# Cached samples on a table of uneven slots, four value pages a visit, and value rows spread by GpSimd

## The chip, the cores and the metric

One core of a Trainium2 chip runs the kernel. The metric is the device time of one execution in microseconds; lower is better. TensorE (PE in the profile), VectorE (DVE), ScalarE (ACT), GpSimd (POOL) and the DMA queues work at the same time, and each engine runs its own instruction list in order.

## The reference, cut to what matters

One step of a decoder layer, for a prompt of 256 tokens and for 8 samples of one token each (264 tokens together). Every token is projected by one large weight matrix. From the projections come two branches, attention with 8 heads and an mLSTM memory with 4 heads, which are gated, projected again and added to the input.

```python
xn = rms_norm(x, norm_w)
aq, ak, av, az, mq, mk, mv, mo, mz, ga, gm, mi, mf = split(xn @ w_in)
# attention of a sample over its 1024 cached tokens (8 pages of 128): the 3 best of 4 blocks of 256
gate = einsum(q, mean of each block's keys);  keep the top 3 blocks
p = softmax([q . k of the kept blocks, q . k_new]);  out = p @ [v, v_new]
# mLSTM, one sample (one token), per head:  C is 256 x 256, n is 256
c_new = a_prev * C + a_s * outer(k, v)          # all 8 samples x 4 heads are written back
n_new = a_prev * n + a_s * k
h     = (w_inter * q @ C + s * v) / max(|den|, exp(-m))
# mLSTM, prompt: the same over 256 tokens with decay weights w[s, t] (a cumulative sum along the row)
y = x + (sigmoid(ga) * ((attn * silu(az)) @ w_proj_attn) + sigmoid(gm) * ((h * silu(mz)) @ w_proj_mlstm)) @ w_out
```

The whole matrix is in fp32: 112 chunks of weights (1024 x 128, 512 KB each) are read once, and the keys and values of 64 pages (512 KB each) once.

## The kernel before, in words

Everything is laid out channel by token. A chunk of weights gives 128 channels of 264 tokens: the weights are split into a rounded part `whi` (ScalarE, L818) and the rest `wlo` (VectorE, L1071), and `project` (L506 to L538) does 16 matmuls with `whi` and 8 with `wlo`. One chunk is one **slot** here. The first 8 chunks are the query heads. Then come 64 slots of the body (g = 0 to 63, in four rounds j of 16, i = g modulo 16), and 40 slots of the tail (g = 64 to 103; i = 0 to 39 in the code of the tail).

Beside the projections each engine does the rest of the work at fixed slots, written out by hand in each engine's loop. On TensorE the extra work of two body slots is done together behind the projection of the odd slot (`beside`, L721, called at L743 to L748); in the tail it follows each slot (L790).

- **A round j** makes one mLSTM head and two attention heads (`keys_side`, `states_side`). At i = 8 TensorE reads the eight old states of the head against the samples' queries (L639), and at i = 9 it transposes the samples' value vectors, 8 rows of 256 (L645), and sums the prompt's normaliser (L652). ScalarE copies the value rows out twice, as fp32 and as rounded (L937, L938), VectorE makes the remainder (L1294, `mvs2`), and TensorE then spreads each sample's row over all 128 partitions by a matmul with a picked unit column (L689): four pairs of samples at i = 11, 12, 13 and 14, in the PSUM banks wk[0], wk[3], wk[0] and wk[2]. VectorE's `new_states` (L1245) takes the row from PSUM, multiplies it with the sample's key column and adds the faded old state (L1252), at i = 12, 13, 15 and at the next round's i = 0.
- **A cached sample b** has its eight key pages scored by VectorE, one a slot (`score_page`, L1162), from slot 2 + 9b. The lags SUMS to GATHER (L86) say what follows: sums on TensorE (L705), the choice of blocks on VectorE (`select`), a maximum over partitions on GpSimd (L462), shift, exp on ScalarE (`cache_probs`, L874), and the values on TensorE (L717), two pages a visit, four visits at lags 13, 15, 17 and 19. `gather` (L878) copies the result out.
- **GpSimd** issues the loads of key and value pages (L404). A key page may be loaded when VectorE has scored the one four pages back, and a value page when TensorE has used the one eight back. It also spreads the samples' query rows (L420) and the two decay rows of a round (L433, L434), which it first fetches from DRAM into partition 0 by DMA (L428, L429).

In-order waits tie these together: TensorE's norms at i = 1 and 3 of a round wait for `new_states` of the round before (L573, L576), since they write the same PSUM banks.

## Time and profile before

| | |
|---|---|
| median of 3 runs | 469.39 us (469.06 to 470.25) |
| span of the profiled execution | 467.2 us, 11345 instructions |
| PE, DVE, ACT, POOL busy | 456.2, 394.1, 294.4, 100.9 us |
| granted TensorE clock | 1.000 (2.4 GHz) over the whole span |
| DMA | 150.91 MB, mean 323 GB/s |

Of the profiled execution only the span, from its first to its last instruction, is known; its own time is not listed. The median of the timed runs is 2.2 us above that span.

The profile's rows give start and length of an instruction or of a run of equal ones. A matmul's end is modelled and reaches into the next, so lengths are read here from start to start. An fp32 matmul shows as two records, a rounded one (`project`) or a transpose as one.

### The profile page before, as it was taken

How to read it: one execution, taken by the hardware profiler on the slowest of the kernel's cores; microseconds unless marked ns; L12 is line 12 of the kernel's file. 1: busy time of each engine (PE TensorE's matmuls, PEld its weight loads, DVE VectorE, ACT ScalarE, POOL GpSimd, SP SyncE). 2: the span in 40 equal slices, each digit the busy share in tenths (PEclk: the TensorE clock that was granted, in tenths of full speed). 3: DMA queues.
4: the chain of work that ended last, by engine and by line, in shares of the span. 5: the costliest groups of instructions: out<-in, count | busy, mean ns of one | idle time of the engine just before them, and what ended most of it. 6: DMA issues, size and time to landing. Idle time of an engine off the chain costs nothing.

```text
span 467.2 us, 11345 instructions
## 1 busy us (share of the span) xinstructions
PE 456.2 (98%) x3855; PEld 413.8 (89%) x3855; DVE 394.1 (84%) x1610; ACT 294.4 (63%) x490; POOL 100.9 (22%) x181
## 2 busy tenths in 40 slices
PE   6999999999999999999999999999999999999997
PEld 4899899897879888888899889899898898899997
DVE  3898899699999799999899999799999774668861
ACT  4966545686984496995486695666948357324430
POOL 2040421013323213423321332321223110000000
PEclk9999999999999999999999999999999999999999
DMA  8899699749999999999999999998999985457511
GB/s 304 322 353 407 183 322 371 240 158 340 317 416 408 404 368 354 412 410 408 408 380 315 409 412 409 411 372 303 382 415 409 410 334 188 149 180 261 182 48 48
DMA packets 44858, 150.91 MB, mean 323 GB/s; under 512 B 6192, under 2 KB 7796, under 8 KB 44672
## 3 DMA queue, kind: packets, MB, share of 16 engines
q1 hardware_dynamic: 20368, 70.77, 40.8%
q0 software_dynamic: 19008, 67.20, 37.3%
q10 hardware_dynamic: 5424, 12.21, 6.8%
q8 instruction: 31, 0.51, 0.4%
q14 instruction: 27, 0.22, 0.1%
HBM read 137.37 MB, written 12.76 MB: 321 GB/s over the span
## 4 chain that ended last, share of the span: by engine, by line
PE 70%; ACT 10%; DVE 10%; DMA 4%; issue 4%; ACTq 1%; POOLq 0%; SPq 0%; POOL 0%; DVEq 0%
PE pj L534 28%; PE pj L537 13%; PE wk L534 6%; PE pa L717 4%; PE wk L537 3%; DMA kpages<-in_cache_k 3%; DVE kpages L1170 3%; DVE wlo L1071 2%; ACT L838 2%; ACT whi L818 2%; PE wk L487 2%; DVE cslot L1252 2%; PE wk L639 2%; PE wk L673 1%; DMA cst<-in_consts 1%
## 5 line engine op out<-in xcount | busy, mean ns | idle before, releaser
L534 PE MATMUL pj<-xn,whi 128*128 128x264 f32 x1328 | 180.8, 288 | 1.6 <-ACT mqT L976 1.3
L534 PEld LDWEIGHTS pj<-xn,whi 128*128 128x128 f32 x1328 | 168.4, 189 | 10.2 <-issue 6.2
L1071 DVE TENSOR_TENSOR wlo<-wraw,whi 128x1024 fp32r<-128x1024 f32 x112 | 136.1, 1220 | 8.8 <-ACT whi L818 8.3
L818 ACT ACTIVATE whi<-wraw 128x1024 fp32r<-128x1024 f32 x112 | 117.9, 1053 | 23.1 <-PE wk L537 12.9
L1170 DVE CUSTOM_DVE_ANT_0 kpages<-kpages,qbc 128x128 f32<-128x128 f32 x512 | 115.5, 292 | 5.3 <-DMA kpages<-in_cache_k 5.1
L537 PE MATMUL pj<-xn,wlo 128*128 128x264 f32 x664 | 93.8, 284 | 0.4 <-DVE wlo L1071 0.4
L537 PEld LDWEIGHTS pj<-xn,wlo 128*128 128x128 f32 x664 | 85.5, 188 | 0.6 <-DVE wlo L1071 0.6
L404 POOL DMA_DIRECT2D kpages<-in_cache_k x64 | 34.3, 536 | 165.9 <-DVE sco L1170 141.9
L404 POOL DMA_DIRECT2D vpages<-in_cache_v x64 | 33.9, 530 | 57.9 <-issue 38.9
L1170 DVE DVE_READ_ACCUMULATOR2_ANT sco<- 128x1 f32 x512 | 42.8, 84 | 0.0
L717 PE MATMUL pa<-vpages,prob 128*32 128x256 f32 x512 | 34.2, 385 | 1.7 <-ACT prob L876 1.7
L1252 DVE SCALAR_TENSOR_TENSOR cslot<-wk,kc,cslot 128x256 f32<-128x256 f32 x64 | 26.5, 478 | 1.7 <-PE wk L689 1.7
L534 PE MATMUL wk<-xn,whi 128*128 128x264 f32 x192 | 26.0, 288 | 0.0
L534 PEld LDWEIGHTS wk<-xn,whi 128*128 128x128 f32 x192 | 24.2, 189 | 1.6 <-issue 1.6
L717 PEld LDWEIGHTS pa<-vpages,prob 128*32 128x32 f32 x512 | 13.4, 109 | 13.6 <-issue 3.1
L866 ACT ACTIVATE cslot<-cslot,bcg 128x512 f32<-128x512 f32 x32 | 21.2, 711 | 0.0
L911 ACT ACTIVATE att<-att,rsum 128x128 f32<-128x128 f32 x8 | 3.2, 403 | 25.7 <-DVE rsum L1233 25.7
L534 PE MATMUL wk<-mlg,whi 128*128 128x264 f32 x128 | 17.0, 285 | 0.0
L534 PEld LDWEIGHTS wk<-mlg,whi 128*128 128x128 f32 x128 | 16.0, 188 | 0.5 <-issue 0.4
L534 PE MATMUL pj<-mlg,whi 128*128 128x264 f32 x112 | 14.9, 285 | 0.0
L534 PEld LDWEIGHTS pj<-mlg,whi 128*128 128x128 f32 x112 | 14.0, 188 | 0.8 <-issue 0.4
L537 PE MATMUL wk<-xn,wlo 128*128 128x264 f32 x96 | 13.5, 283 | 0.0
(271 smaller groups left out, 615.0 us busy)
## 6 DMA issues: line engine op xcount, KB each, us to landing
wraw<-in_weights SPq DMA_DIRECT2D x112, 512.0 KB, 6.8
kpages<-in_cache_k POOLq DMA_DIRECT2D x64, 512.0 KB, 8.1
vpages<-in_cache_v POOLq DMA_DIRECT2D x64, 512.0 KB, 10.8
cslot<-in_states SPq DMA_DIRECT2D x16, 512.0 KB, 9.4
out_C_s<-cslot ACTq DMA_DIRECT2D x16, 512.0 KB, 8.1
xres<-in_tokens SPq DMA_DIRECT2D x1, 1056.0 KB, 5.5
out_k_p<-kT ACTq DMA_DIRECT2D x4, 256.0 KB, 10.2
out_v_p<-v_nat ACTq DMA_DIRECT2D x4, 256.0 KB, 4.7
```

Source lines behind the costliest of these rows:

```text
L404: return pool.dma_start(tile, src)
L487: return nc.tensor.transpose(out, in_, ident[0:rows_, 0:rows_])
L534: mm(bank[:, 0:T], whi[:, q, k, :], src[:, g, k, :], start=(k == 0 and g == 0), stop=False)
L537: last = mm(bank[:, 0:T], wlo[:, n % WRAW, k, :], src[:, 0, k, :], start=False, stop=(k == KC - 1))
L639: mm(wk[1][g * VC:(g + 1) * VC, 0:MHD], qmask[:, d, b * VC:(b + 1) * VC], cslot[:, b, d, :], start=(half == 0 and d == 0), stop=(half == 1 ...
L717: last = mm(pv[q * VC:(q + 1) * VC, 0:VW], prob[:, b % 2, first:first + VC], vpages[:, s % VSLOTS, q * VW:(q + 1) * VW], start=(pg == 0), ...
L818: A(whi[:, n % WSPLIT], wraw[:, n % WRAW], ACT.Copy).then_inc(whi_ready, 1)
L838: ch.link(A(dst, ss, ACT.Ln, scale=1.0 / width, bias=epsc))
L866: A(cslot[:, b], cslot[:, b], ACT.Copy, scale=bcg[:, 0, j, b:b + 1]).then_inc(fade_ready, 1)
L1071: V.tensor_tensor(wlo[:, n % WRAW], wraw[:, n % WRAW], whi[:, n % WSPLIT], ALU.subtract).then_inc(wlo_ready, 1)
L1170: last = V.tensor_tensor_reduce(k, k, qbc[:, b % 2, h * HD:(h + 1) * HD], 1.0, 0.0, ALU.mult, ALU.add, sco[:, b % 2, pg, h:h + 1])
L1252: last = V.scalar_tensor_tensor(out=cslot[:, b, d, :], in0=row, scalar=kc[:, d, b:b + 1], in1=cslot[:, b, d, :], op0=ALU.mult, op1=ALU.add)
```

## The change

- **The samples' table.** `due`, `key_page` and the pairs of value pages no longer follow one period. Samples 0 to 5 start at slots 2, 12, 20, 30, 38 and 48, with the same lags as before; samples 6 and 7 have their keys over slots 58 to 66 and 68 to 78, and their other steps listed by hand. Values come in two visits of four pages, at 13 and 17 slots after the start, and for samples 6 and 7 at 74 and 77, 83 and 84. Value pages are loaded one a slot by a table of its own (`LOADS`).
- **Value rows.** The broadcasts by matmul (L689), the split (L938, L1294) and the two small transposes (L645) go. At i = 8 TensorE makes sixteen matmuls of 32 x 128 with the identity, each of a quadrant of 32 partitions, so that quadrant q of wk[3] holds the rows of samples 2q and 2q + 1. ScalarE copies that once into `mvq`, and GpSimd spreads one quadrant's first row (512 numbers) over 128 partitions into `mvb`, four times a round: two at i = 10, one at i = 12, one at i = 13. `new_states` reads the row from `mvb` in SBUF, no longer from PSUM.
- **Decay rows** are put once at the start into partitions 0, 32, 64 and 96 of a tile `stage`, by one DMA, and spread from there at i = 13; the DMAs of each round through DRAM go.
- **Order and waits.** The normaliser's sums (L652) go before the new matmuls in wk[1]; `nnew` is copied by VectorE (it was ScalarE). TensorE's norms wait for `pT_ready` and `cn_ready` of the round before, no longer for `new_states`. In the tail the tokens' scores move from slot 3 to 8 (TensorE), their VectorE part from 12 to 18, their exp from 14 to 19, the totals from 18 to 20. Some waits of GpSimd for its own results are added. The mask of the attention shares one copy, so the constants are 128 columns shorter.

```diff
-START, PERIOD = 2, 9
-SUMS, SELECT, SHIFT, EXP, VALUES, TOTAL, GATHER = 9, 10, 11, 12, 13, 14, 20
+SUMS, SELECT, SHIFT, EXP, TOTAL, GATHER = range(6)
+LAGS = (9, 10, 11, 12, 14, 20)
+STARTS = [2, 12, 20, 30, 38, 48]
+KEYS = [[s + p for p in range(PAGES)] for s in STARTS] + [[58, 59, 60, 61, 62, 63, 64, 66], [68, 69, 71, 72, 74, 75, 77, 78]]
+STEPS = [[s + lag for lag in LAGS] for s in STARTS] + [[68, 69, 70, 71, 72, 80], [79, 80, 81, 81, 82, 85]]
+VISITS = [[s + 13, s + 17] for s in STARTS] + [[74, 77], [83, 84]]
+LOADS = [[]] + [[s + 14 + p for p in range(PAGES)] for s in STARTS] + [[75, 76, 76, 77, 78, 78, 79, 79]]
...
-            def decay_rows(j):
+            def spread_rows(j):
...
-                pool.dma_start(wt[0:1, 0:SEQ], rows_dram[j:j + 1, 0:SEQ]).then_inc(row_load, 16)
-                pool.dma_start(emt[0:1, :], rows_dram[j:j + 1, SEQ:2 * SEQ]).then_inc(row_load, 16)
...
+                row = stage[j * VC:j * VC + 1, :]
+                nc.gpsimd.partition_broadcast(wt[:, 0:SEQ], row[:, 0:SEQ]).then_inc(row_spread, 1)
+                nc.gpsimd.partition_broadcast(emt, row[:, SEQ:2 * SEQ]).then_inc(row_spread, 1)
+                pool.wait_ge(row_spread, 2 * (j + 1))
+
+            def spread_values(j, c):
+
+                pool.wait_ge(mv_ready, 2 * j + 2)
+                if c >= 2:
+                    pool.wait_ge(c_ready, NB * j + 2 * (c - 1))
+                elif j:
+                    pool.wait_ge(c_ready, NB * (j - 1) + 2 * (c + 3))
+                nc.gpsimd.partition_broadcast(mvb[:, c % 2, 0:2 * MHD], mvq[c * VC:c * VC + 1, :]).then_inc(v_spread, 1)
+                pool.wait_ge(v_spread, VG * j + c + 1)
...
-                        pe.wait_ge(c_ready, NB * j - 2) if j else pe.wait_ge(q_ready, HEADS)
+                        pe.wait_ge(pT_ready, 2 * j) if j else pe.wait_ge(q_ready, HEADS)
...
-                        pe.wait_ge(c_ready, NB * j) if j else pe.wait_ge(qs_ready, 2)
+                        pe.wait_ge(cn_ready, j) if j else pe.wait_ge(qs_ready, 2)
...
-                    for n in range(2):
-                        last = tr(wk[3][0:NB, n * P:(n + 1) * P], rawT[:, n, SEQ:T], P)
-                    last.then_inc(mvtr_ps, 1)
...
+                    for pick in range(2):
+                        for n in range(2):
+                            c = pick * MHD + n * P
+                            for q in range(VG):
+                                col = SEQ + 2 * q + pick
+                                last = mm(wk[3][q * VC:(q + 1) * VC, c:c + P], rawT[:, n, col:col + 1].broadcast_to([P, VC]), ident,
+                                          start=True, stop=True)
+                    last.then_inc(mvtr_ps, 1)
...
-                if i in (11, 12, 13, 14):
-                    pair = i - 11
-                    bank = (wk[0], wk[3], wk[0], wk[2])[pair]
...
-                    for n in range(2):
-                        last = mm(bank[:, n * MHD:(n + 1) * MHD], eye2[:, 2 * pair + n:2 * pair + n + 1].broadcast_to([P, P]),
-                                  mvs2[:, :], start=True, stop=True)
-                    last.then_inc(vbc_ps, 1)
...
-                    for pg in (2 * pair[1], 2 * pair[1] + 1):
+                    for pg in range(many * p, many * (p + 1)):
...
+                    act.wait_ge(mvtr_ps, 2 * j + 2)
+                    act.wait_ge(v_spread, VG * j)
+                    A(mvq[:, :], wk[3][:, :], ACT.Copy).then_inc(mv_ready, 1)
...
-                    A(mvs, wk[3][0:NB, 0:MHD], ACT.Copy)
-                    A(mvs2[0:NB, :], wk[3][0:NB, 0:MHD], ACT.Copy).then_inc(mv_ready, 1)
-                    A(nnew[:, j, :], wk[3][:, MHD:MHD + MHD // VG], ACT.Copy).then_inc(n_ready, 1)
...
-                    dve.wait_ge(vbc_ps, 4 * j + b // 2 + 1)
-                    row = (wk[0], wk[3], wk[0], wk[2])[b // 2][:, b % 2 * MHD:(b % 2 + 1) * MHD]
+                    dve.wait_ge(v_spread, VG * j + b // 2 + 1)
+                    row = mvb[:, b // 2 % 2, b % 2 * MHD:(b % 2 + 1) * MHD]
...
+                    V.tensor_copy(nnew[:, j, :], wk[1][:, NNEW:NNEW + MHD // VG]).then_inc(n_ready, 1)
...
-                if i == 10:
-                    dve.wait_ge(mv_ready, 2 * j + 2)
-                    V.tensor_tensor(mvs2[LO:LO + NB, :], mvs, mvs2[0:NB, :], ALU.subtract).then_inc(mvlo_ready, 1)
```

How the instructions stand now. First TensorE behind the projection of slot 25 (second round, i = 8 and 9), in the kernel before; L639 reads the old states, L717 is a visit of two value pages, L645's transposes show under the helper's line L487 as `8x128`, and L652 is the normaliser:

```order
L487 MATMUL wk<-cst,att 128x128 x3
L487 MATMUL wk<-cst,sq 128x128 x4
L639 MATMUL wk<-cslot,qmask 32x256 x16
L641 MATMUL wk<-qsum,cst 128x16
L717 MATMUL pa<-vpages,prob 32x256 x8
L487 MATMUL wk<-cst,sq 8x128 x2
L652 MATMUL wk<-mk_nat,decay 32x64 x8
```

The same place in the changed kernel, with its own line numbers (L654 is the reading of the states, L670 the new matmuls, L721 a visit):

```order
L502 MATMUL wk<-cst,att 128x128 x3
L502 MATMUL wk<-cst,sq 128x128 x4
L654 MATMUL wk<-cslot,qmask 32x256 x16
L661 MATMUL wk<-mk_nat,decay 32x64 x8
L670 MATMUL wk<-cst,sq 32x128 x16
L673 MATMUL wk<-qsum,cst 128x16
L721 MATMUL pa<-vpages,prob 32x256 x16
```

The two transposes have become sixteen narrow matmuls, and the visit has twice as many matmuls.

Then TensorE in the tail, slots 78 to 80 of the kernel before, where L534 and L537 are projections:

```order
L534 MATMUL wk<-xn,whi 128x264 x16
L537 MATMUL wk<-xn,wlo 128x264 x8
L717 MATMUL pa<-vpages,prob 32x256 x8
L534 MATMUL wk<-xn,whi 128x264 x16
L537 MATMUL wk<-xn,wlo 128x264 x8
L534 MATMUL pj<-mlg,whi 128x264 x16
L537 MATMUL pj<-mlg,wlo 128x264 x8
L717 MATMUL pa<-vpages,prob 32x256 x8
```

And slots 83 and 84 of the changed kernel (L549 and L552 are projections, L766 the totals):

```order
L549 MATMUL wk<-mlg,whi 128x264 x16
L552 MATMUL wk<-mlg,wlo 128x264 x8
L721 MATMUL pa<-vpages,prob 32x256 x16
L549 MATMUL pj<-mlg,whi 128x264 x16
L552 MATMUL pj<-mlg,wlo 128x264 x8
L766 MATMUL wk<-lsum,cst 128x64
L721 MATMUL pa<-vpages,prob 32x256 x16
```

The tail had ten visits of two pages and has five of four.

Last GpSimd at the end of the first round, before (L420 spreads a query row, L428 and L429 fetch the decay rows, L433 and L434 spread them, L401 and L404 issue a page):

```order
L420 ISA qbc<-qbc 128x1024
L428 DMA decay<-rows_dram 1x16x16
L429 DMA floor<-rows_dram 1x16x16
L401 TENSOR_LOAD ptab
L401 ISA x2
L404 ISA
L404 DMA kpages<-in_cache_k 128x1024
L433 ISA decay<-decay 128x256
L434 ISA floor<-floor 128x256
```

and now, from slot 12 to 13 (L448 spreads two value rows, L437 and L438 the decay rows):

```order
L448 ISA mvb<-mvq 128x512
L408 TENSOR_LOAD ptab
L408 ISA x2
L411 ISA
L411 DMA kpages<-in_cache_k 128x1024
L448 ISA mvb<-mvq 128x512
L437 ISA decay<-stage 128x256
L438 ISA floor<-stage 128x256
```

The value rows' broadcasts stand between the loads of pages, and the decay rows need no DMA.

## Rows read from the trace of the kernel before

**Rows 1.** Page, part 1: busy time, share of the span, instructions
```profile
PE 456.2 (98%) x3855; PEld 413.8 (89%) x3855; DVE 394.1 (84%) x1610; ACT 294.4 (63%) x490; POOL 100.9 (22%) x181
```

**Rows 2.** Waits of TensorE in body and tail: us in total, times, longest
```profile
PE pa L717 <- ACT prob L876: 1.7, 3, 0.7
PE pj L534 <- ACT mqT L976: 1.3, 2, 0.7
...
PE pj L537 <- DVE wlo L1071: 0.4, 1, 0.4
```

**Rows 3.** Timeline of TensorE, slots 77 to 80: start us, length us
```profile
379.95 2.12 PE L534 MATMUL pj<-xn,whi 128*128 128x264 f32 x16
...
382.88 2.12 PE L534 MATMUL wk<-xn,whi 128*128 128x264 f32 x16
...
385.89 1.07 PE L717 MATMUL pa<-vpages,prob 128*32 128x256 f32 x16
386.89 2.23 PE L534 MATMUL wk<-xn,whi 128*128 128x264 f32 x16
...
389.93 2.12 PE L534 MATMUL pj<-mlg,whi 128*128 128x264 f32 x16
```

**Rows 4.** Timeline of TensorE, value rows of the third round, first and last pair
```profile
243.24 0.58 PE L689 MATMUL wk<-mvs,eye 128*128 128x256 f32 x2
243.66 2.13 PE L534 MATMUL pj<-xn,whi 128*128 128x264 f32 x16
...
258.33 0.40 PE L689 MATMUL wk<-mvs,eye 128*128 128x256 f32 x2
258.56 1.05 PE L696 MATMUL wk<-sq,cst 128*128 128x264 f32 x4
```

**Rows 5.** Timeline of TensorE, i = 8 and 9 of the fourth round
```profile
301.38 1.93 PE L639 MATMUL wk<-cslot,qmask 128*32 128x256 f32 x32
303.25 0.40 PE L641 MATMUL wk<-qsum,cst 128*128 128x16 f32 x2
...
303.74 0.38 PE L487 MATMUL wk<-cst,sq 128*8 128x128 f32 x2
304.05 0.43 PE L652 MATMUL wk<-mk_nat,decay 128*32 128x64 f32 x16
304.30 1.05 PE L717 MATMUL pa<-vpages,prob 128*32 128x256 f32 x16
```

**Rows 6.** Timeline of GpSimd, broadcasts of 256 and of 1024 numbers a partition
```profile
52.90 0.55 POOL L434 PARTITION_BROADCAST floor<-floor  x1
...
53.84 2.35 POOL L451 PARTITION_BROADCAST qbc<-qs  x1
...
157.28 1.45 POOL L420 PARTITION_BROADCAST qbc<-qbc  x1 [6.37 <-DMA qbc<-q_dram]
```

**Rows 7.** Timeline of VectorE, under the last of these
```profile
157.28 0.29 DVE L1170 CUSTOM_DVE_ANT_0 kpages<-kpages,qbc 128x128 f32<-128x128 f32 x1
...
157.49 1.24 DVE L1170 CUSTOM_DVE_ANT_0 kpages<-kpages,qbc 128x128 f32<-128x128 f32 x1
```

**Rows 8.** Groups of instructions, VectorE: busy us, mean ns, idle before
```profile
L1170 DVE CUSTOM_DVE_ANT_0 kpages<-kpages,qbc 128x128 f32<-128x128 f32 x512 | 115.5, 292 | 5.3 <-DMA kpages<-in_cache_k 5.1
L1252 DVE SCALAR_TENSOR_TENSOR cslot<-wk,kc,cslot 128x256 f32<-128x256 f32 x64 | 26.5, 478 | 1.7 <-PE wk L689 1.7
L1294 DVE TENSOR_TENSOR mvs<-zraw,mvs 8x256 fp32r<-8x256 f32 x4 | 2.0, 506 | 1.9 <-ACT mvs L938 1.9
```

**Rows 9.** Timeline of TensorE, slot 15
```profile
109.81 1.25 PE L537 MATMUL pj<-xn,wlo 128*128 128x264 f32 x8 [0.39 <-DVE wlo L1071]
```

**Rows 10.** Timeline of ScalarE, slots 30 to 34
```profile
187.48 0.39 ACT L881 ACTIVATE accr<-pa 128x256 f32<-128x256 f32 x1 [2.22 <-PE pa L717]
...
203.99 0.37 ACT L976 ACTIVATE mqT<-pj 128x264 f32<-128x264 f32 x1
```

**Rows 11.** Loads of pages by GpSimd (L404)
```profile
DMA to landing us min/median/max: 4.3/9.5/16.9
```

More of the change, by code:

```diff
@@ L77, with due, value_visit, value_loads @@
 VC = 32
+NNEW = MHD + VC
 BODY = JOBS * CHUNKS
 LAST = BODY + 5 * KC
-START, PERIOD = 2, 9
-SUMS, SELECT, SHIFT, EXP, VALUES, TOTAL, GATHER = 9, 10, 11, 12, 13, 14, 20
-def due(g, lag):
-    b, left = divmod(g - START - lag, PERIOD)
-    return b if left == 0 and 0 <= b < NB else None
-def key_page(g):
-    b, pg = divmod(g - START, PERIOD)
-    return b * PAGES + pg if 0 <= b < NB and pg < PAGES else None
-def value_pair(g):
-    for p in range(PAGES // 2):
-        b = due(g, VALUES + 2 * p)
-        if b is not None:
-            return b, p
-    return None
+SUMS, SELECT, SHIFT, EXP, TOTAL, GATHER = range(6)
[5 more added lines that the diff above has]
+LOADS = [[]] + [[s + 14 + p for p in range(PAGES)] for s in STARTS] + [[75, 76, 76, 77, 78, 78, 79, 79]]
+def due(g, step):
+    for b in range(NB):
+        if g == STEPS[b][step]:
+            return b
+    return None
+def key_page(g):
+    for b in range(NB):
+        if g in KEYS[b]:
+            return b * PAGES + KEYS[b].index(g)
+    return None
+def value_visit(g):
+    for b in range(NB):
+        for p, slot in enumerate(VISITS[b]):
+            if g == slot:
+                return b, p, PAGES // len(VISITS[b])
+    return None
+def value_loads(g):
+    return [b * PAGES + p for b in range(1, NB) for p in range(PAGES) if g == LOADS[b][p]]
 class Chain:
@@ L320, in build @@
         q_dram = nc.dram_tensor("q_dram", (NB, D), F32, kind="Internal").ap()
-        rows_dram = nc.dram_tensor("rows_dram", (MH, 2 * SEQ), F32, kind="Internal").ap()
         block = ctx.enter_context(nc.Block())
@@ L443, in _ @@
             pool.wait_ge(rows_ready, 1)
-            pool.dma_start(rows_dram, rows[:, :, :].rearrange("p a t -> p (a t)")).then_inc(row_put, 16)
+            pool.dma_start(stage[ds(0, MH, step=VC), :], rows[:, :, :].rearrange("p a t -> p (a t)")).then_inc(row_put, 16)
             pool.wait_ge(row_put, 16)
-            decay_rows(0)
             spread_rows(0)
@@ L470, in _ @@
                         spread_queries(s // PAGES + 1)
-                pair = value_pair(g)
-                if pair is not None:
-                    for s in range(pair[0] * PAGES + 2 * pair[1] + VSLOTS, pair[0] * PAGES + 2 * pair[1] + VSLOTS + 2):
-                        if s < NB * PAGES:
-                            values(s)
+                for s in value_loads(g):
+                    values(s)
+                if g < BODY and g % CHUNKS == 10:
+                    spread_values(g // CHUNKS, 0)
+                    spread_values(g // CHUNKS, 1)
+                if g < BODY and g % CHUNKS in (12, 13):
+                    spread_values(g // CHUNKS, g % CHUNKS - 10)
                 if g % CHUNKS == 13 and g // CHUNKS + 1 < JOBS:
-                    decay_rows(g // CHUNKS + 1)
-                if g % CHUNKS == 14 and g // CHUNKS + 1 < JOBS:
                     spread_rows(g // CHUNKS + 1)
@@ L640, in states_side @@
                                    start=(half == 0 and d == 0), stop=(half == 1 and d == EC - 1))
[L641 to L646 removed]
+                    pe.wait_ge(w_ready, j + 1)
                     part = MHD // VG
@@ L651, in states_side @@
                         for q in range(VG):
-                            last = mm(wk[3][q * VC:(q + 1) * VC, MHD:MHD + part], wt[:, col:col + 1].broadcast_to([P, VC]),
+                            last = mm(wk[1][q * VC:(q + 1) * VC, NNEW:NNEW + part], wt[:, col:col + 1].broadcast_to([P, VC]),
                                       mk_nat[:, t, q * part:(q + 1) * part], start=(t == 0), stop=(t == 1))
                     last.then_inc(n_ps, 1)
+                    pe.wait_ge(sw_ready, j + 1)
+                    for pick in range(2):
[6 more added lines that the diff above has]
+                    last.then_inc(mvtr_ps, 1)
+                    mm(wk[1][:, MHD:MHD + 2 * NB], ones, qsum[:, :, :], start=True, stop=True).then_inc(qc_ps, 1)
                 if i == 10:
@@ L705, in cache_side @@
                     mm(page_sums[b % 2], ones, sco[:, b % 2].rearrange("p a h -> p (a h)"), start=True, stop=True).then_inc(g_ps, 1)
-                pair = value_pair(g)
-                if pair is not None:
-                    b = pair[0]
-                    if pair[1] == 0:
+                visit = value_visit(g)
+                if visit is not None:
+                    b, p, many = visit
+                    if p == 0:
                         pe.wait_ge(prob_ready, b + 1)
                         pe.wait_ge(accr_ready, b)
-                    for pg in (2 * pair[1], 2 * pair[1] + 1):
+                    for pg in range(many * p, many * (p + 1)):
                         s = b * PAGES + pg
@@ L1402, in _ @@
                     merged_values()
[L1403 removed]
+                if i == 18:
                     token_scores()
```

69 lines of the change are left out of this document (23 added, 46 removed).

## The prediction

> **What bounds the kernel now.** I read the page's busy times first, then TensorE's waits, then its timeline from start to start, and last the engines that could take its place. TensorE is busy for 456.2 of 467.2 us, VectorE for 394.1, GpSimd for 100.9 [rows 1]. From the body on TensorE stands still for only 1.7 + 1.3 + 0.4 = 3.4 us in six waits of note, of which 3.0 us are waits for ScalarE [rows 2]. So two things can shorten this kernel: less work on TensorE, which counts in full wherever no other engine is late, and those 3.4 us. VectorE is close behind. In slot 15 TensorE waited for the weight remainder `wlo` [rows 9], so there VectorE had no lead left at all; it is the engine to fear.
>
> The profiled span is 467.2 us and the median of the runs 469.39. I make the sum against the span and carry the 2.2 us between them over unchanged.
>
> **Value rows: what TensorE loses and gains.** Eight matmuls L689 a round go. The first pair of the third round takes 243.66 - 243.24 = 0.42 us, the last 258.56 - 258.33 = 0.23 [rows 4]; the two between take 0.4 and 0.34, about 1.4 us a round and 5.6 in all. Not all of it is gained. L689 is of the same rounded kind as the projections, and softens the change between kinds. The cost of such a change shows in the tail: a slot alone lasts 382.88 - 379.95 = 2.93 us, the one that follows an fp32 visit 389.93 - 386.89 = 3.04, so 0.11 [rows 3]. Two to three places a round now pay it: 0.3 a round, 1.2 in all. The two transposes take 304.05 - 303.74 = 0.31 a round, 1.2 in all [rows 5].
>
> Added are sixteen fp32 matmuls of 32 x 128 a round. The trace has none of that shape. The nearest rows are those of L639, also 32 partitions wide, four quadrants in turn: sixteen of 256 columns in 303.25 - 301.38 = 1.87 us [rows 5]. Half the columns gives 0.94. L717 gives the same, eight of 256 columns in 386.89 - 385.89 = 1.00 [rows 3], so 1.0. From below, eight of 64 columns (L652) take 0.25 [rows 5], so sixteen take 0.5 if columns don't count. From above, if the quadrants did not overlap, each would cost what one of the two transposes does, 0.155, so 2.5 a round. I take 0.95, since L639 is the row that it is nearest to: 3.8 in all, between 2 and 10. Value rows together: -5.6 + 1.2 - 1.2 + 3.8 = -1.8 us, between -3.6 and +4.4.
>
> **Visits.** 32 visits of two pages become 16 of four; the matmuls stay 256. In the tail the slots 78 and 79 with a visit take 389.93 - 382.88 = 7.05 us against 2 x 2.93 = 5.86, so a visit of 1.00 brings 0.19 of change with it [rows 3]. Ten such visits stand in the tail before and five after: -0.95. In the body 22 become 11, all behind other fp32 work that pays most of the change anyway. I take 0.1 each, between 0 and 0.19: -1.1 (0 to -2.1). Visits together -2.0 us.
>
> **Waits.** The waits for ScalarE are at the seams of the rounds, where it has a chain of table loads. In the second seam it first waited 2.22 us at L881 for a visit of TensorE, then worked without a pause until the evacuation L976 at 203.99 that TensorE was waiting for [rows 10]. `gather` of that sample moves from slot 31 to 32 behind a visit of slot 29, so this wait goes, though its copy and two DMA issues now stand in the crowded slot. The exp of sample 6 (slot 68) goes to 72, off its visit. In the first seam ScalarE waits for VectorE's hidden state, and VectorE has no key page in slots 10 and 11 where it had one in 11. But both seams are chains on ScalarE, and what TensorE saves ahead of them is partly lost in waiting for them: about 1.5 us of value rows and visits lies in the stretches before. Of the 3.4 us I count 0.8 gained net; between 3.4 gained and nothing, with the TensorE savings there lost as well (+1.5).
>
> **VectorE.** It loses L1294, 2.0 us, and the wait ahead of it, 1.9, and the waits of L1252 for L689, 1.7 [rows 8]. Of the 56 key pages that it scored in the body 54 are left, which is 2 x 8 x 0.21 = 3.4 us (0.21 from start to start, 157.28 to 157.49 [rows 7]). It gains four copies of 64 columns, under 1 us together. I cost this at nothing because TensorE's own work hides it, save in slots like 15.
>
> Against it stand sixteen new broadcasts on GpSimd. One of 256 numbers takes 0.55 us, one of 1024 took 2.35 from another tile and 1.45 in place [rows 6]; 512 numbers lie between, 0.8 by the row in place. What such a broadcast does to VectorE the trace shows once clearly. Under L420 at 157.28 a scoring instruction took 1.24 us, where the mean is 0.29 [rows 6, 7, 8], so 0.95 lost. From below it is nothing, when VectorE is waiting anyhow or reads PSUM. I take 0.45 each, about half of the one row as the broadcast has half the length: 7.2 us against the 8 us of relief, so no net change. VectorE's L1252 reads its row from SBUF now instead of PSUM; its length (0.478) I leave alone.
>
> On this the Trainium skill has a rule that speaks against the change (SBUF — State Buffer, "Who interferes with whom"): a VectorE instruction with two SBUF inputs contends with a GpSimd instruction that reads SBUF, and whichever comes first locks the other out for its whole length. The stretched row agrees, as both of its inputs are in SBUF. By the rule L1252, whose row came from PSUM, joins those that can be locked out, and every broadcast that meets VectorE costs it what is left of the broadcast.
>
> **GpSimd's own queue.** The new broadcasts wait for ScalarE's copy (slot 10) and for `new_states` (slots 12, 13). Behind them in the queue are page loads. A key page is loaded four pages ahead and takes 4.3 to 16.9 us, 9.5 in the middle [rows 11]. Value pages of samples 2 and 4 are loaded only four slots before their visit. A slot lasts at least 2.93 us [rows 3], so they have at least 11.7 us and, with the work beside the projections, more. I cost it at nothing; if that cover is gone, a visit waits up to 16.9 - 11.7 = 5.2 us. GpSimd is 22% busy and eight DMAs of its queue go. The table's effect on ScalarE is two table loads fewer, in the tail where it waits for TensorE anyway: nothing. The end after the last projection is untouched, and so is the start, but for 64 KB of constants.
>
> **Sum.** -1.8 - 2.0 - 0.8 = -4.6 us. Span 462.6, time 464.8 us.
>
> **Rivals.**
> - *VectorE is held up by the broadcasts, and TensorE by it (slower).* For it: rows 7, and slot 15 without a lead [rows 9]. The place is i = 10 to 14 of each round, four broadcasts. At 0.95 each they cost 3.8 us a round, against 0.9 of L1294 with its wait and 0.85 of a key page; the 2.0 that is left reaches TensorE through `wlo`, 8 in all. With -3.8 of less work: +4.2, 473.6 us. The break-even is at (3.8 + 7.0) / 16 = 0.68 us a broadcast; above that the kernel is slower. Against it: VectorE is idle for some of that time, and two of the four come before the point at i = 11 where it waits for TensorE.
> - *ScalarE's seams set the rounds (no change).* For it: 3.0 of 3.4 us of waits are for ScalarE, and it is not relieved. Then the savings of the body become waits at the seams, and the tail's 0.95 alone is sure: 468.4 us. Against it: no single one of these waits is over 0.7 us.
> - *The waits go as well (faster still).* VectorE's free slots 10, 11, 28, 29, 46 and 47 put the hidden state and the shift early: -3.8 - 3.4 = -7.2, 462.2 us.
> - *Late value pages.* Two visits wait some 3 us each: -4.6 + 6 = +1.4, 470.8 us. Against it: before, pages landed in 9.5 us in the middle, and no visit waited for a DMA.
>
> **How the numbers follow.** Forecast 0.58 (463.4 to 467), the seams 0.13, the waits too 0.15, VectorE held up 0.11, late pages 0.03. Less or more than 0.3% (1.4 us) is what a measurement of this kernel can tell from no change. Faster: 0.58 + 0.15 and a share of the seams' case that saves more than 1.4 us, 0.77. Same 0.11, slower 0.12. The range of 80% runs from 461.8, the forecast with its waits gone, to 468.6, the seams' case. It leaves out most of the slower cases and the best ends of the value rows.
>
> **What would show it.** Right: no L689; the sixteen new matmuls of a round in about 0.95 us from start to start; visits of 2.0 us, 0.19 of change each, five in the tail; TensorE busy for about 452 of 463 us; its waits in the body no more than 3 us. Wrong: the new matmuls in 2 us or more; VectorE instructions of over 1 us under most of the L448 broadcasts, with waits of TensorE for `wlo`; waits of visits for a page; or waits at `mqT` or `prob` of more than 3.4 us together.

## The result, and the profile after

The changed kernel takes 475.61 us (median, 474.25 to 477.23) against 469.82 for the kernel before in the same comparison: ratio 1.0128, 95% interval 1.0107 to 1.015. The forecast was 464.8 us, the range 461.8 to 468.6. The sign is wrong and the time lies outside the range. The profiled execution took 475.26 us, its span 473.6.

The page of the changed kernel, parts 1 and 2, answers to [rows 1]: busy us, share of the span and instructions; then the granted clock of TensorE in 40 slices of 11.8 us, in tenths.

```profile
PE 454.1 (96%) x3943; PEld 418.1 (88%) x3943; DVE 397.7 (84%) x1610; ACT 291.7 (62%) x480; POOL 117.2 (25%) x185
...
PEclk9999999999999999997999999899999999999999
```

TensorE is busy for 2.1 us less than before, not 4, and there are two slices in which it ran at a lower clock. Its waits in the body and the tail, to be laid beside [rows 2] (us in total, times, longest):

```profile
PE pa L721 <- DMA vpages<-in_cache_v: 6.2, 2, 3.2
PE pa L721 <- ACT prob L881: 2.5, 2, 1.9
...
PE pj L552 <- DVE wlo L1074: 1.3, 3, 0.6
PE pj L549 <- ACT sq L839: 1.3, 1, 1.3
PE pj L549 <- ACT mqT L979: 1.1, 1, 1.1
...
PE wk L502 <- ACT att L917: 0.2, 1, 0.2
```

They sum to 12.6 us. Before, the same kinds of wait came to 3.8: the three of [rows 2], and two of 0.2 us. The first line is new. No visit waited for a page before; now two do, three microseconds each. The timeline of TensorE around them (start us, length us, and in brackets what it waited for):

```profile
206.12 2.12 PE L549 MATMUL pj<-xn,whi 128*128 128x264 f32 x16
208.08 1.13 PE L552 MATMUL pj<-xn,wlo 128*128 128x264 f32 x8
...
209.80 1.50 PE L721 MATMUL pa<-vpages,prob 128*32 128x256 f32 x24
214.32 1.08 PE L721 MATMUL pa<-vpages,prob 128*32 128x256 f32 x8 [3.02 <-DMA vpages<-in_cache_v]
215.33 3.89 PE L549 MATMUL pj<-xn,whi 128*128 128x264 f32 x16
219.02 1.72 PE L552 MATMUL pj<-xn,wlo 128*128 128x264 f32 x8
220.58 2.10 PE L549 MATMUL pj<-xn,whi 128*128 128x264 f32 x16
...
297.45 1.50 PE L721 MATMUL pa<-vpages,prob 128*32 128x256 f32 x24
302.18 1.08 PE L721 MATMUL pa<-vpages,prob 128*32 128x256 f32 x8 [3.23 <-DMA vpages<-in_cache_v]
303.19 3.31 PE L549 MATMUL pj<-xn,whi 128*128 128x264 f32 x16
306.34 1.13 PE L552 MATMUL pj<-xn,wlo 128*128 128x264 f32 x8
```

Three pages of the visit are used (x24), then TensorE stands still for the fourth: the last page of sample 2, and of sample 4. What follows is slow too. From start to start the sixteen L549 after the first wait take 219.02 - 215.33 = 3.69 us, the eight L552 1.56; after the second wait the L549 take 3.15. In a kernel below, in which the first wait is short, the same rows take 2.07 and 0.97, and the last eight matmuls of the visit 0.57 instead of 1.01. So after each wait some matmuls ran at the lower of the two clock levels, 1.2 instead of 2.4 GHz (the granted clock from 215.33 to 219.02 is 0.50 of full speed), and that cost (3.69 - 2.07) + (1.56 - 0.97) + (3.15 - 2.07) + 2 x (1.01 - 0.57) = 4.2 us. The windows of the trace show the granted clock there (length, busy time with instructions, clock as a share, DMA share, GB/s):

```profile
192.00:208.00 16.00, 14.85 (x131) 1.00 1.03 414
208.00:224.00 16.00, 12.98 (x99) 0.79 1.02 408
288.00:304.00 16.00, 12.77 (x109) 0.94 1.03 410
304.00:320.00 16.00, 16.00 (x183) 0.95 0.90 354
```

The span grew by 6.4 us: waits +8.8, lower clock +4.2, and so TensorE's own work -6.6. I call what is left of a span without those waits and that clock the kernel's work: 463.4 us before, 456.8 after. It is good to a few tenths only, since a listed wait leaves out what the matmuls lose at its edges (a case is read below, under the value rows alone). The work was forecast to shrink by 3.8 and shrank by more.

Why the page was late stands in GpSimd's timeline. These are slots 32 and 33:

```profile
196.18 0.53 POOL L411 DMA_DIRECT2D kpages<-in_cache_k  x1 [3.06 <-DVE sco L1173]
196.73 1.30 POOL L427 PARTITION_BROADCAST qbc<-qbc  x1
199.25 0.55 POOL L411 DMA_DIRECT2D vpages<-in_cache_v  x1 [1.22 <-issue]
201.67 0.53 POOL L411 DMA_DIRECT2D kpages<-in_cache_k  x1 [1.87 <-DVE sco L1173]
202.81 0.54 POOL L411 DMA_DIRECT2D vpages<-in_cache_v  x1 [0.61 <-issue]
```

The last two lines are slot 33: a key load that waits until VectorE has scored the page in its buffer (`sco`), and behind it the value load for slot 37. It leaves at 202.81 and lands at about 214.2, which is 11.4 us, a usual time for a page ([rows 11]: 9.5 in the middle, up to 16.9; the value pages of the changed kernel alone: 10.9 in the middle). TensorE wants it at 211.3. GpSimd keeps step with VectorE, and VectorE is some slots behind TensorE: TensorE had ended its visit of slot 33 at 194.93. The "four slots ahead" of the table are four slots in the order of the code; in time they were 8.5 us.

### The profile page after: what moved, and what is told of

It reads as the page before. It is cut to its first block, busy times and chain, and to the rows that moved or that the text cites. A ratio compares the mean times of both kernels' runs of the same rounds, so it can differ in the third digit from the quotient of the medians.

```text
span 473.6 us, 11533 instructions
## 1 busy us (share of the span) xinstructions
PE 454.1 (96%) x3943; PEld 418.1 (88%) x3943; DVE 397.7 (84%) x1610; ACT 291.7 (62%) x480; POOL 117.2 (25%) x185
## 4 chain that ended last, share of the span: by engine, by line
PE 70%; DVE 13%; ACT 6%; DMA 6%; issue 3%; POOL 1%; POOLq 0%; ACTq 0%; SPq 0%; DVEq 0%
PE pj L549 26%; PE pj L552 13%; PE wk L549 8%; DMA vpages<-in_cache_v 5%; PE pa L721 4%; PE wk L552 4%; DVE kpages L1173 3%; DVE wlo L1074 3%; PE wk L502 2%; DVE cslot L1255 2%; PE wk L654 2%; ACT L843 1%; ACT whi L823 1%; PE wk L558 1%; PE wk L557 1%
## 5 line engine op out<-in xcount | busy, mean ns | idle before, releaser
L549 PE MATMUL pj<-xn,whi 128*128 128x264 f32 x1328 | 184.4, 292 | 2.4 <-ACT sq L839 1.3
L549 PEld LDWEIGHTS pj<-xn,whi 128*128 128x128 f32 x1328 | 171.6, 191 | 9.6 <-issue 4.5
L1173 DVE CUSTOM_DVE_ANT_0 kpages<-kpages,qbc 128x128 f32<-128x128 f32 x512 | 118.9, 296 | 0.9 <-DMA kpages<-in_cache_k 0.7
L552 PE MATMUL pj<-xn,wlo 128*128 128x264 f32 x664 | 94.6, 285 | 1.3 <-DVE wlo L1074 1.3
L552 PEld LDWEIGHTS pj<-xn,wlo 128*128 128x128 f32 x664 | 86.1, 189 | 2.0 <-DVE wlo L1074 2.0
L1173 DVE DVE_READ_ACCUMULATOR2_ANT sco<- 128x1 f32 x512 | 41.2, 81 | 0.0
L721 PE MATMUL pa<-vpages,prob 128*32 128x256 f32 x512 | 32.2, 390 | 8.8 <-DMA vpages<-in_cache_v 6.2
L721 PEld LDWEIGHTS pa<-vpages,prob 128*32 128x32 f32 x512 | 15.1, 110 | 20.6 <-DMA vpages<-in_cache_v 7.2
L1255 DVE SCALAR_TENSOR_TENSOR cslot<-mvb,kc,cslot 128x256 f32<-128x256 f32 x64 | 27.2, 485 | 0.0
L549 PE MATMUL wk<-xn,whi 128*128 128x264 f32 x192 | 25.8, 287 | 0.0
L549 PEld LDWEIGHTS wk<-xn,whi 128*128 128x128 f32 x192 | 24.3, 189 | 1.2 <-issue 1.2
L549 PE MATMUL wk<-mlg,whi 128*128 128x264 f32 x128 | 17.1, 286 | 0.0
L448 POOL PARTITION_BROADCAST mvb<-mvq x16 | 16.5, 1032 | 0.8
L549 PEld LDWEIGHTS wk<-mlg,whi 128*128 128x128 f32 x128 | 16.2, 189 | 0.1
L1287 DVE COPY qcs<-wk 128x256 f32<-128x256 f32 x4 | 1.7, 422 | 17.2 <-PE wk L673 17.2
L549 PE MATMUL pj<-mlg,whi 128*128 128x264 f32 x112 | 15.1, 287 | 0.0
## 6 DMA issues: line engine op xcount, KB each, us to landing
vpages<-in_cache_v POOLq DMA_DIRECT2D x64, 512.0 KB, 10.9
```

The source lines that it names most:

```text
L448: nc.gpsimd.partition_broadcast(mvb[:, c % 2, 0:2 * MHD], mvq[c * VC:c * VC + 1, :]).then_inc(v_spread, 1)
L549: mm(bank[:, 0:T], whi[:, q, k, :], src[:, g, k, :], start=(k == 0 and g == 0), stop=False)
L552: last = mm(bank[:, 0:T], wlo[:, n % WRAW, k, :], src[:, 0, k, :], start=False, stop=(k == KC - 1))
L721: last = mm(pv[q * VC:(q + 1) * VC, 0:VW], prob[:, b % 2, first:first + VC], vpages[:, s % VSLOTS, q * VW:(q + 1) * VW], start=(pg == 0), ...
L1173: last = V.tensor_tensor_reduce(k, k, qbc[:, b % 2, h * HD:(h + 1) * HD], 1.0, 0.0, ALU.mult, ALU.add, sco[:, b % 2, pg, h:h + 1])
L1255: last = V.scalar_tensor_tensor(out=cslot[:, b, d, :], in0=row, scalar=kc[:, d, b:b + 1], in1=cslot[:, b, d, :], op0=ALU.mult, op1=ALU.add)
```

## The experiments

Two theories at the start. A: the two late pages, with the clock behind them, are the loss. B: the broadcasts hold VectorE up, and TensorE waits behind it. Ratios are to the kernel before, beside which each kernel ran (469.25 to 469.76 us), with 95% intervals. Diffs are against the changed kernel or the kernel before, as said.

### Value loads two a slot (against the changed kernel)

```diff
-LOADS = [[]] + [[s + 14 + p for p in range(PAGES)] for s in STARTS] + ...
+LOADS = [[]] + [[s + 14 + p // 2 + p // 4 * 2 for p in range(PAGES)] for s in STARTS] + ...
```

> The changed kernel with its value pages loaded two a slot instead of one (the first four of a sample at 14 and 15 slots after the start of the one before, the last four at 18 and 19), so that the last page has two slots more before its visit. Late-pages theory: the two waits for a value page (6.2 us) go, and with them the stretches of 1.2 GHz behind them (about 3.3 us by the rows of the changed kernel): 475.6 - 9.5 = about 466 us, clock 1.00. Broadcast theory (VectorE held up by GpSimd): nothing of its cost changes, 474 us or more.

467.92 us, ratio 0.9959 (0.9937 to 0.9981): 7.7 us faster than the changed kernel, and faster than the kernel before. No visit waits for a page and the clock stays up. A holds for most of the loss, though 2 us more stayed than I expected.

### The value rows alone (the changed kernel with the old table)

```diff
+STARTS = [2 + 9 * b for b in range(NB)]
+VISITS = [[s + 13, s + 15, s + 17, s + 19] for s in STARTS]
+LOADS = [[]] + [[VISITS[b][p // 2] for p in range(PAGES)] for b in range(NB - 1)]
 (KEYS, STEPS and the tail's steps as before the change)
```

> The changed kernel with the table of the kernel before (period of 9, visits of two pages, loads at the visits, tail steps at their old slots): only the value rows by GpSimd, the staged decay rows and the looser waits are new. Late-pages theory: no visit waits for a page; TensorE has some 1.8 us less work, and the broadcasts cost nothing: 466 to 468.5 us. Broadcast theory: the loss is here, 473 us or more.

471.34 us, 1.0024 (1.0009 to 1.004). I had expected 466 to 468.5 from A and 473 or more from B; it is neither. Its first line of waits is this:

```profile
PE pj L552 <- DVE wlo L1074: 4.7, 8, 1.1
```

### The same without the broadcasts

```diff
-                nc.gpsimd.partition_broadcast(mvb[:, c % 2, 0:2 * MHD], mvq[c * VC:c * VC + 1, :]).then_inc(v_spread, 1)
-                pool.wait_ge(v_spread, VG * j + c + 1)
+                pool.sem_inc(v_spread, 1)
 (and mvb is set to zero once at the start)
```

> As the run with the old table and the new value rows, but without the sixteen broadcasts of value rows: the semaphore is raised, the copy in SBUF stays at zero, so the outer product of the samples' new states is left out of the result. The difference to that run is the price of the broadcasts. Late-pages theory: under 0.5 us. Broadcast theory: 4 us or more faster than that run.

468.45 us, 0.9973 (0.996 to 0.9987), and the line is now

```profile
PE pj L552 <- DVE wlo L1074: 1.1, 1, 1.1
```

The sixteen broadcasts cost 471.34 - 468.45 = 2.9 us, and TensorE's listed waits for `wlo` fall from 4.7 to 1.1. B is real too, at 0.18 us a broadcast. It stands below the 4 us that B named, above the 0.5 of A. The list shows such a wait too short. At the second one (0.57 us, slot 17) a projection and the `wlo` matmuls behind it last 121.05 - 117.28 = 3.77 us from start to start, without the broadcasts 2.92, so 0.85 is lost. By this, a part of what the broadcasts cost hides in what I call work.

### The new table alone, value rows by matmul (against the kernel before)

```diff
-START, PERIOD = 2, 9
+STARTS = [2, 12, 20, 30, 38, 48]
 (KEYS, STEPS, VISITS and LOADS as in the changed kernel)
```

> The kernel before with the changed kernel's table (starts, keys, visits of four pages, loads one a slot, tail steps), and its value rows still by matmul. Late-pages theory: the loss is here, waits for value pages at the visits of slots 37 and 55 of some 3 us each and a lower clock behind them: 469.8 - 2 + 9.5 = about 477 us. Broadcast theory: 467 to 468 us.

472.91 us, 1.0082 (1.0055 to 1.0109). The waits for `vpages` are here as well:

```profile
PE pa L728 <- DMA vpages<-in_cache_v: 4.8, 2, 3.5
```

So the table makes them, not the broadcasts. I had expected about 477: the first wait is 3.45 us and the clock falls behind it (the next sixteen matmuls take 3.26 us), but the second is only 1.33 and nothing is slow after it.

### The new table with value loads two a slot, value rows by matmul

```diff
 (the kernel above)
+LOADS = [[]] + [[s + 14 + p // 2 + p // 4 * 2 for p in range(PAGES)] for s in STARTS] + ...
```

> The kernel before with the new table of samples and visits and four pages a visit, value rows still by a matmul on TensorE, and the value loads put out two a slot so that the last of a visit leaves GpSimd at least two slots earlier. Two-cause theory (late pages cost 7.7 us between the changed kernel and the one with early pages, broadcasts 2.9 us): no wait of a visit for vpages, clock 1.0 throughout, no wlo wait over 1.5 us in sum, time 465 to 467. Rival, that the table's bunched samples (slots 2, 12, 20, 30, 38, 48) have a price of their own on ScalarE and VectorE: 468.5 or more with longer waits for prob and sq.

476.88 us, 1.0154 (1.0129 to 1.0178): a clear miss, 10 us above the range that I expected. The same mend that gave 7.7 us with the value rows on GpSimd cost 4.0 here. TensorE waited once for 7.4 us for `wlo`. GpSimd's timeline shows behind what (then VectorE's):

```profile
262.42 0.53 POOL L418 DMA_DIRECT2D vpages<-in_cache_v  x1 [0.73 <-PE pa L728]
262.96 0.50 POOL L442 DMA_DIRECT2D decay<-rows_dram  x1
263.45 0.49 POOL L443 DMA_DIRECT2D floor<-rows_dram  x1
277.88 0.54 POOL L447 PARTITION_BROADCAST decay<-decay  x1 [13.94 <-DMA floor<-rows_dram]
```
```profile
278.87 0.42 DVE L1273 TENSOR_TENSOR decay<-decay,cst 128x256 f32<-128x256 f32 x1 [10.80 <-POOL floor L448]
```

The decay rows of the next head, 1 KB each, are fetched by GpSimd's queue just behind four value pages and a key page of 512 KB each. GpSimd waits 13.94 us for the second of them. Before, the longest of these landings was 7.9 us and VectorE lost 1.6 in all to them. This is the third part of the change, which I had priced at nothing: the staged rows are in SBUF from the start and fetch nothing.

### Visits of four pages alone, two loads a slot (against the kernel before)

```diff
+STARTS = [2 + 9 * b for b in range(NB)]
+VISITS = [[s + 13, s + 17] for s in STARTS]
+LOADS = [[]] + [[s + 14 + p // 2 + p // 4 * 2 for p in range(PAGES)] for s in STARTS]
 ...
```

> The kernel before with one thing of the change: the two visits of two pages a period become one of four pages, loads two a slot, samples, value rows and tail as before. By the prediction's term for the visits (0.1 us each in the body and 0.19 in the tail) about 2 us less than before, 467.7. Rival: the visits' saving is hidden because TensorE's next block then waits for ScalarE or VectorE instead: 469 to 470, with prob or wlo waits over 5 us in sum.

479.77 us, 1.0226 (1.0191 to 1.0261), a miss of 12 us and of both theories' numbers. The decay rows again: GpSimd waited 6.59 and 11.45 us for them in two rounds, VectorE 3.45 and 4.27 us, TensorE 3.00 and 4.95 us for `wlo`.

### Value load ahead of the key load in a slot (against the changed kernel)

```diff
+                for s in value_loads(g):
+                    values(s)
                 if s is not None:
                     if s + KSLOTS < NB * PAGES:
                         keys(s + KSLOTS)
 ...
-                for s in value_loads(g):
-                    values(s)
```

> The changed kernel with its own table of loads, but in each GpSimd slot the value load stands ahead of the key load, which waits for VectorE. If the page is late because it is queued behind that wait: the two waits for vpages fall from 3 us each to about 1 us each and the clock stays at 1.0, time 470 to 472. If the page is late because the DMA engines share their rate among too many transfers: waits and time unchanged, 475 to 476.

466.74 us, 0.9937 (0.9917 to 0.9957): faster than I expected of this mend. The waits for `vpages` are 0.9 us together and the clock stays at 1.0. Nothing is loaded earlier by the table and no byte fewer is moved, so it was the wait of the key load for VectorE ahead of it in the queue that made the page late. The DMA engines' rate has a part in it all the same: the load of slot 33 leaves at 199.65, 3.16 us earlier than in the changed kernel, and TensorE has the page only 2.2 us earlier (212.13 against 214.32).

### Two page loads one slot earlier (against the changed kernel)

```diff
+LOADS[2][7], LOADS[4][7] = LOADS[2][7] - 1, LOADS[4][7] - 1
```

> The changed kernel with two of its 56 later value loads one slot earlier (page 7 of sample 2 from slot 33 to 32, page 7 of sample 4 from slot 51 to 50), nothing else. If those two pages carry the loss (waits of 3.0 and 3.2 us, and about 3.3 us of matmuls at the lower clock after them): both waits under 0.5 us, clock 1.0, time 466.5 to 469. Rival, that the pages are late because the DMA engines are full, so that others become late instead: 472 or more, or new waits for vpages or kpages.

466.7 us, 0.9957 (0.9941 to 0.9974), with clock 1.0. The waits for the two pages are 0.79 and 0.53 us, a little over the 0.5 that I expected. Two of 56 loads moved by a slot give back 8.9 us. GpSimd's row of the load, then TensorE's of the visit:

```profile
200.43 0.53 POOL L412 DMA_DIRECT2D vpages<-in_cache_v  x1 [0.61 <-issue]
```
```profile
212.12 0.64 PE L722 MATMUL pa<-vpages,prob 128*32 128x256 f32 x8 [0.79 <-DMA vpages<-in_cache_v]
212.69 2.23 PE L550 MATMUL pj<-xn,whi 128*128 128x264 f32 x16
214.76 1.13 PE L553 MATMUL pj<-xn,wlo 128*128 128x264 f32 x8
215.73 0.53 PE L550 MATMUL pj<-xn,whi 128*128 128x264 f32 x3
```

The load leaves 202.81 - 200.43 = 2.38 us earlier and the wait shrinks from 3.02 to 0.79, by 2.23. Here the L550 take 214.76 - 212.69 = 2.07 us, the L553 0.97 and the last page 0.57, the measure used above for the clock's price. Its waits from the body on are 7.8 us, so its work is 464.5 - 7.8 = 456.7, within 0.1 of what was worked out for the changed kernel with the clock's 4.2 us taken off (456.8). That closes the account.

### Both mends together (against the changed kernel)

```diff
 (LOADS two a slot, and value loads ahead of the key load)
```

> The changed kernel with both mends: value loads two a slot and ahead of the key load in GpSimd's slot. The kernel with the order alone measured 466.7 and still waited 0.9 us for vpages; that with two a slot 467.9 and 1.3 us for v_nat. If the mends add: 465.5 to 466.5, no wait for vpages. Rival, that earlier value pages only push key pages and query rows back: 467 to 469, with more idle time of VectorE for kpages than 9.8 us.

474.51 us, 1.0101 (1.0062 to 1.014). The mends do not add; the rival was right in kind and too mild. VectorE now stands still for `kpages` for 13.9 us against 9.8 with the loads two a slot and 7.5 with the order alone, and TensorE behind it, with the lower clock after two of its waits (0.993 over the span):

```profile
PE pj L552 <- DVE wlo L1074: 3.7, 4, 2.4
PE wk L670 <- DVE decay L1282: 3.0, 1, 3.0
```

### Without broadcasts in the new table (against value loads two a slot)

```diff
-                nc.gpsimd.partition_broadcast(mvb[:, c % 2, 0:2 * MHD], mvq[c * VC:c * VC + 1, :]).then_inc(v_spread, 1)
-                pool.wait_ge(v_spread, VG * j + c + 1)
+                pool.sem_inc(v_spread, 1)
 (and mvb is set to zero once at the start)
```

> The changed kernel with early pages and without the 16 broadcasts of the samples' value rows on GpSimd; the samples' outer product of each head is left out on VectorE's side of it as far as it reads them, so this is a price and not a version. If the broadcasts cost VectorE's followers in the new table what they cost in the old one (2.9 us): 465.0 from 467.9. Rival, that the new table gives VectorE room and nothing waits for it: 467.5 to 468.

465.7 us, 0.9919 (0.9896 to 0.9943), so the broadcasts cost 467.92 - 465.7 = 2.2 us here, 0.14 each; between the two theories' numbers, nearer to the first.

### Staged decay rows added to the two that lost most, and alone

```diff
-                pool.dma_start(wt[0:1, 0:SEQ], rows_dram[j:j + 1, 0:SEQ]).then_inc(row_load, 16)
-                pool.dma_start(emt[0:1, :], rows_dram[j:j + 1, SEQ:2 * SEQ]).then_inc(row_load, 16)
+                row = stage[j * VC:j * VC + 1, :]
+                nc.gpsimd.partition_broadcast(wt[:, 0:SEQ], row[:, 0:SEQ]).then_inc(row_spread, 1)
+                nc.gpsimd.partition_broadcast(emt, row[:, SEQ:2 * SEQ]).then_inc(row_spread, 1)
 ...
```

In the new table with two loads a slot (476.88 us without):

> The new table with two value pages a slot, value rows still by a matmul on TensorE, and now the staged decay rows: one DMA of all four heads' rows at the start instead of two DMAs a head in GpSimd's queue behind the value pages. Theory that the 476.9 us without staging came from the rows landing 14 us late (VectorE 10.8 us for floor, TensorE 7.4 us for wlo, then a stretch at the lower clock): no wait of VectorE for floor over 1 us, no wlo wait over 1 us, clock 1.0, time 465 to 467.5. Rival, that these pages and samples hold VectorE up whatever brings the decay rows: over 472. Against the kernel with early pages and broadcasts (467.9) it also prices the value rows: below 467 if the broadcasts' hold is dearer than the matmuls they take away, above 469 if not.

468.08 us, 0.9966 (0.9947 to 0.9984), 8.8 us faster, 0.6 above the range that I expected, and within 0.2 of the same loads with the value rows on GpSimd (467.92). VectorE's wait for `floor` is gone, the longest wait for `wlo` is 1.1 us instead of 7.4, the clock is 1.0.

In the kernel with visits of four pages alone (479.77 us without):

> The kernel before with visits of four pages and two value loads a slot (479.8 us) plus the staged decay rows. If the late decay rows are all that was wrong with it: 467 to 468.5, as the prediction's term for the visits has it. Rival: the visits cost by themselves, over 471.

469.11 us, 0.999 (0.9975 to 1.0005), 10.7 us faster, 0.6 above what I expected: of the work saved, part became waits for `prob` (3.5 us, 1.7 before) and `wlo` (2.4, 0.4 before).

Alone in the kernel before:

> The kernel before with the staged decay rows and nothing else. In the kernel before VectorE waits for floor for 1.6 us in two times and TensorE hardly for wlo (0.4 us), so I expect 469.2 to 469.9, no difference. Rival, that the two DMAs a head cost the loads behind them something: 468.5 or less.

468.72 us, 0.999 (0.9971 to 1.0009), no difference that can be told, though 0.5 under the range that I expected. The staged rows are worth little or nothing with the loads of the kernel before, whose decay rows land in 7.9 us at most. With value pages two a slot ahead of them they took up to 14.3 us (new table) and 11.9 (visits alone).

### New table, staged rows, values first, value rows by matmul

```diff
 (the first of the three above, LOADS one a slot as in the changed kernel)
+                for s in value_loads(g):
+                    values(s)
                 (ahead of keys)
```

> The new table and visits with staged decay rows, value rows by a matmul as in the kernel before, value loads one a slot but ahead of the key load. Against the kernel with the same order and broadcasts (466.7) it prices the value rows a second time: two slots a page earlier they were worth nothing (468.1 with matmuls, 467.9 with broadcasts), so 466 to 467.5 here. Rival, that in this order VectorE has no slack and the broadcasts were the dearer: under 465.5.

464.88 us, 0.9909 (0.9892 to 0.9926), the fastest of all. Its page, part 1, and its waits:

```profile
PE 451.6 (97%) x3855; PEld 416.6 (90%) x3855; DVE 395.6 (85%) x1610; ACT 291.9 (63%) x488; POOL 95.3 (21%) x173
```
```profile
PE pa L723 <- ACT prob L882: 1.8, 1, 1.8
...
PE pj L540 <- ACT sq L840: 1.3, 1, 1.3
PE pj L540 <- ACT mqT L982: 1.1, 1, 1.1
PE pj L543 <- DVE wlo L1077: 0.6, 1, 0.6
...
PE wk L493 <- ACT att L918: 0.2, 1, 0.2
```

It is under the 465.5 of the rival. Beside the same order with broadcasts (466.74) it has 463.3 - 5.0 = 458.3 us of work where that has about 457.1, and 5.0 us of waits where that has 7.7. So moving the value rows to GpSimd takes 1.2 us off TensorE here and gives it back, or more, as waits. The medians are 1.9 us apart but the ratios' intervals overlap (0.9892 to 0.9926, 0.9917 to 0.9957), and with the loads two a slot there was no difference (468.08, 467.92). The change's first idea is worth nothing, perhaps a little less; which of the two isn't settled.

## Why the prediction was wrong

**The step that failed** is in "GpSimd's own queue": "Value pages of samples 2 and 4 are loaded only four slots before their visit. A slot lasts at least 2.93 us [rows 3], so they have at least 11.7 us [...] I cost it at nothing". Two things were wrong in it. The slots were counted on TensorE, but the load is issued by GpSimd, behind a key load that follows VectorE; the lead was 211.3 - 202.81 = 8.5 us, under the 9.5 of a middling landing. The load left 202.81 - 194.93 = 7.9 us after TensorE had ended its own visit of that slot. The idle time of GpSimd before its key loads, most of it waiting for `sco`, was there to be read in the groups of the kernel before:

```profile
L404 POOL DMA_DIRECT2D kpages<-in_cache_k x64 | 34.3, 536 | 165.9 <-DVE sco L1170 141.9 <-issue 24.0
```

The rival "late value pages" named the mechanism, the number of visits and 3 us each exactly, and got 0.03; and it priced only the waits. The clock after them adds 4.2 us to its 6.2. Mended alone, at two loads, this step is 8.9 us of the 10.8 between forecast and result. The 1.9 us that stay are the waits below, 4.8 us worse than forecast, less the work, 2.9 better.

The range was also summed loosely: the forecast with its waits gone is 462.2 us and not 461.8, the seams' case 468.4 and not 468.6. It doesn't matter for the result.

**Value rows**, forecast -1.8 (-3.6 to +4.4): the work falls by 458.3 - 456.7 = 1.6 us between the last kernel above and the one with two loads moved. In the old table it falls by 463.0 - 461.2 = 1.8 us from the staged rows alone to the kernel without broadcasts, and not at all with them (463.1). The nearest row was the right one:

```profile
313.06 1.06 PE L670 MATMUL wk<-cst,sq 128*32 128x128 f32 x32
314.05 0.40 PE L673 MATMUL wk<-qsum,cst 128*128 128x16 f32 x2
```

The new matmuls take 314.05 - 313.06 = 0.99 us a round, forecast 0.95.

**Visits**, forecast -2.0: mis-sized, to the good. The visits of four pages alone, with staged rows, have 467.2 - 7.8 = 459.4 us of work against 463.4 before, so -4.0, or -3.6 against the staged rows alone (463.0). Each visit of four is shorter than two of two. In the changed kernel's tail:

```profile
387.67 1.93 PE L721 MATMUL pa<-vpages,prob 128*32 128x256 f32 x32
389.53 2.22 PE L549 MATMUL wk<-xn,whi 128*128 128x264 f32 x16
```

That is 1.86 us, not 2 x 1.00 [rows 3]: 0.14 for each of sixteen, 2.2 us that I left out. The table beyond the visits gives 1.1 more (458.3 against 459.4), with the tail's moved steps in it, which no run has alone.

**Waits**, forecast -0.8 net: wrong in sign. The waits for ScalarE rose from 3.2 (3.0 in [rows 2] and one of 0.2) to 5.1 us. The visit of slot 51 waits 1.84 to 1.86 us for `prob` in eight of the ten kernels with the new table, since ScalarE comes to this `prob` only at the end of its chain of table loads there. The seams' rival fits this: work saved ahead of a seam is waited for at the seam. No run relieves ScalarE, so that stays an argument. The kernel with two loads moved has no long page wait: work -6.7, waits +4.0 (1.3 of them for pages), and so a span of -2.7 instead of -4.6.

**VectorE**, forecast no net cost with 0.45 us a broadcast: in the one place read below a hold has that size, but that is luck. Over all sixteen VectorE's busy time grows by 2.8 us in the new table (394.6 without the broadcasts, 397.4 with them, loads two a slot) and by 5.1 in the old (394.4, 399.5), so 0.18 to 0.32 each and not the 7.2 us of the forecast. And what a hold costs can't be set against relief elsewhere; it counts where VectorE has no slack. The cost in the kernel's time is 2.2 to 2.9 us. It is far from the 8 us of the rival. The timelines of GpSimd and of VectorE in the changed kernel show a broadcast among VectorE's instructions:

```profile
106.63 2.63 POOL L448 PARTITION_BROADCAST mvb<-mvq  x1
...
111.79 0.80 POOL L448 PARTITION_BROADCAST mvb<-mvq  x1
```
```profile
107.18 1.22 DVE L1074 TENSOR_TENSOR wlo<-wraw,whi 128x1024 fp32r<-128x1024 f32 x1
108.31 0.28 DVE L1173 CUSTOM_DVE_ANT_0 kpages<-kpages,qbc 128x128 f32<-128x128 f32 x1
108.52 0.74 DVE L1173 CUSTOM_DVE_ANT_0 kpages<-kpages,qbc 128x128 f32<-128x128 f32 x1
109.19 0.28 DVE L1173 CUSTOM_DVE_ANT_0 kpages<-kpages,qbc 128x128 f32<-128x128 f32 x1
```

Under the broadcast VectorE lost 0.74 - 0.28 = 0.46 us in one instruction, about the 0.45 of the forecast, and the broadcast itself was stretched more, to 2.63 us where the second one took 0.80. The Trainium skill (SBUF — State Buffer, "Who interferes with whom") says that a VectorE instruction with two SBUF inputs and a GpSimd instruction that reads SBUF contend, and that it is an exclusive lock. These rows fit that in both directions, the long `wlo` instruction at its usual 1.22 us beside a stretched broadcast, then the stretched scoring instruction. Which of the two was first can't be read from them.

**Staged decay rows**, forecast nothing: right in the kernel before (no difference), and yet without them the new table with loads two a slot is 8.8 us slower, and visits of four pages alone are 10.7. An edit worth nothing by itself can be what another edit stands on.

## What to carry to other kernels

A lead counted in slots is time on the engine that issues the load. Read there when the load left, and what that engine waits for ahead of it, before trusting the slots on the engine that uses the data. A transfer that someone waits for doesn't belong behind bulk loads in a queue, however small it is; two 1 KB rows behind five pages of 512 KB took 14 us. And where a rival is a wait of some 3 us on TensorE, price the matmuls at the lower clock behind it as well.

## What was not expected of the hardware

- After TensorE had stood still for 3.02 us its next matmuls ran at the lower clock level: sixteen in 3.69 us from start to start instead of 2.07. After 3.23 us it was 3.15. After 2.38 us (both mends together) eight took 1.92 instead of 0.97, at a granted clock of 0.51. After 1.86 us, the wait for `prob`, there was none of it: the next sixteen took 2.06 us (value loads two a slot).
- The queues moved 319 GB/s in the mean, but 408 to 414 GB/s at a DMA share of 1.02 or 1.03 in the windows that hold the two late pages. There the DMA engines are full, and loads of one kind put earlier came at the cost of the other kind (the two mends together). Full engines alone make no page late, though: the kernel before moves 407 to 410 GB/s at 1.02 or 1.03 in three of the same windows, and no visit waits.
- A broadcast of 512 numbers to all partitions took 1.03 us in the mean of sixteen, 0.80 in the middle and 2.63 at most.
